# The gated delta rule stage of a two-block model: spread rows, masks and the order of the recurrence

## The chip, the core and the metric

The kernel runs on one core of a Trainium2 chip. The metric is the device time of one execution in microseconds (us), lowest is best. TensorE (PE) does the matrix products and writes to PSUM, whose eight banks hold 512 fp32 columns each. VectorE (DVE), ScalarE (ACT) and GpSimd (POOL) do elementwise work, SyncE (SP) issues most DMAs.

## The reference

One sequence of 512 tokens with 16 meta tokens goes through a two-layer block (attention, a short convolution, two MLPs), and then, without the meta tokens, through one hybrid mixer. That mixer normalizes its input, projects it, and runs two branches beside each other: a differential attention with 4 heads, and a gated delta rule with 4 heads of dimension 128 in 8 chunks of 64 tokens. Both outputs are gated and go through one output projection. The change concerns the delta rule:

```
g = cumsum(g within a chunk)
decay = exp(where(tril, g[:, None] - g[None, :], -inf))
lower = where(strict, (k * beta) @ k.T * decay, 0)
u, w = triangular_solve(lower + I, [v * beta, k * beta * exp(g)])
qk_intra = where(tril, q @ k.T * decay, 0)
for each chunk:                                  # state is 128x128 per head
    v_new = u - w @ state
    o = (q * exp(g)) @ state + qk_intra @ v_new
    state = state * exp(g_last) + (k * exp(g_last - g)).T @ v_new
```

## The kernel before

Everything is computed in transposed form, channels on partitions and the 512 tokens along a row. All loops are written out by hand for each engine, and engines wait for each other by counting semaphores (`gd.wait(engine, name, count)`). No scheduler moves anything. PE works in the order written.

The stages of the last 300 us, in the order of PE:

- The input projection of the mixer (L430 products). Its last tile gives `rows`, the 4-partition row quantities of the delta rule, one row for each head.
- The differential attention, four heads c = 0 to 3 (`dif_act`, `dif_dve`, `dif_pe`; products L1833, L1835, L1841, L1865). Between its steps ACT and DVE compute the rows in `rows_act` and `rows_dve`: beta, exp(g), -beta exp(g), exp(g_last - g) and the scan G. With k = 0 (in head 0) ACT has 7 operations, with k = 2 (end of head 1) 9. In head 3 `rows_pe` (L1676) turns four rows into columns with 16 products of 4 columns, and DVE copies them to `gcol`.
- `gdn_pe`, `gdn_act`, `gdn_dve`, `gdn_pool`, the delta rule. Keys and values are turned (L2068, L2076) and scaled by columns: `KDEC` and `X1` on ACT (L2175, L2181), `X2` on DVE (L2249), each in 4 operations a head (one for each block of 128 tokens, called j).
- The exponents of the decays: PE spreads row G of head h over 128 partitions with a selection matrix, `hsel` (L2083, 4 rows, fp32), and adds the mask by four products with the identity (L2085, fp32). ACT takes the exponential (L2186).
- The products q k and k k (L2091, L2097), multiplied on DVE with the decays (L2254, L2257). The spread rows beta (L2101) and exp(g) (L2104) multiply them and the queries (L2261, L2264).
- The inverse of the triangular matrix by levels of doubling blocks: POOL masks the first level for all heads (L2240), DVE forms `TT` (L2268), PE turns it (L2108), and then come five levels of three groups of products (L2125, L2132, L2135). POOL masks for heads 0 and 1, DVE for heads 2 and 3 (L2277).
- The solutions (L2140, L2143), evicted by ACT.
- The recurrence over 8 chunks. In each chunk PE does, for all four heads, the product w state (L2152, bank 4+h) and the query product (L2153, bank h). Then DVE adds u to make `vn` (L2306), and PE does for each head the update of the state (L2160, bank 4+h) and the output part (L2162, bank h). These two have only 64 rows, partitions 0 to 63 in an even chunk and 64 to 127 in an odd one. DVE forms the new state (L2315).
- The normalization of the outputs: ACT squares, PE sums over partitions (L2168), ACT takes the inverse root, DVE multiplies (L2326, L2328), ACT and DVE split the result in a high and a low part. The output projection (L430) starts with the blocks of the attention (k = 4 to 7), and its first tile waits until `o_scaled`, signalled by L2326, has released its bank.

A plain fp32 product is two instructions in the profile (two pairs of weight load and matmul). One whose operands are declared fp32r (a rounded form) is one, and the kernel gets precision back by splitting into high and low parts.

## Time and profile before

| | |
|---|---|
| median of 3 runs | 1817.6 us (1816.02 to 1818.84) |
| profiled execution, own time | 1817.29 us |
| its span | 1815.5 us |
| PE busy | 1743.3 us, 96% |
| DVE, ACT, POOL busy | 885.2, 633.8, 142.4 us |
| chain that ended last, by engine | PE 91%, DVE 4%, ACT 3% |
| TensorE clock granted, mean | 0.967 of full |

The profiled execution took 1.79 us more than its span, and lies 0.3 us under the median. A matmul's end is modelled, so starts are better to read than ends. "PEclk" is the granted clock, 1.00 for 2.4 GHz and 0.50 for 1.2 GHz. Times in rows are counted from the start of the span.

### The profile page before, as it was taken

The numbers are of one execution on the slowest core, as the hardware profiler recorded it, in microseconds if no ns is written. First come the engines' busy times: TensorE is split into PE (matmuls) and PEld (weight loads), VectorE is DVE, ScalarE is ACT, GpSimd is POOL, SyncE is SP. The second block draws the span as 40 slices with busy tenths as digits, with TensorE's granted clock in tenths as the row PEclk, the third lists the DMA queues.
The fourth block names the chain that finished last, engine by engine and source line by source line (L and its number), as shares of the span: only waits on it lengthen the run. The fifth ranks groups of instructions, "written<-read, shape, count | busy, mean of one in ns | idle before, by whom it ended". The sixth has DMA issues, their size and how long they took to land.

```text
span 1815.5 us, 27268 instructions
## 1 busy us (share of the span) xinstructions
PE 1743.3 (96%) x11417; PEld 1511.6 (83%) x11417; DVE 885.2 (49%) x1193; ACT 633.8 (35%) x980; POOL 142.4 (8%) x151
## 2 busy tenths in 40 slices
PE   7999898989999999999999999999999999889998
PEld 6997566789999999999887888888877886666987
DVE  5533346455343333565566333444566477534362
ACT  4523424423232222321233222323344465641222
POOL 1000000032000000220023000000231000003200
PEclk9999898999999999999999999999999999967999
DMA  5240001022232222222223232322364760001001
GB/s 177 71 96 5 7 1 47 2 71 93 93 93 93 93 83 89 87 89 93 93 93 93 94 99 97 103 94 92 95 88 70 94 94 18 1 11 47 1 24 70
DMA packets 137545, 129.57 MB, mean 71 GB/s; under 512 B 17633, under 2 KB 135512, under 8 KB 137452
## 3 DMA queue, kind: packets, MB, share of 16 engines
q1 hardware_dynamic: 137250, 128.18, 26.0%
q8 instruction: 69, 1.13, 0.3%
q14 instruction: 24, 0.20, 0.0%
q10 hardware_dynamic: 202, 0.06, 0.0%
HBM read 126.14 MB, written 2.10 MB: 71 GB/s over the span
## 4 chain that ended last, share of the span: by engine, by line
PE 91%; DVE 4%; ACT 3%; issue 1%; SPq 1%; DMA 0%; ACTq 0%; DVEq 0%
PE ps L430 71%; PE ps L859 3%; PE ps L756 1%; PE ps L739 1%; PE ps L1865 1%; PE ps L1090 1%; PE ps L2125 1%; PE ps L2135 1%; PE ps L2132 1%; PE ps L1152 1%; PE ps L2152 0%; PE ps L2160 0%; PE ps L764 0%; SPq L2376 0%; PE ps L2083 0%
## 5 line engine op out<-in xcount | busy, mean ns | idle before, releaser
L403 ACT ACTIVATE w_hi<-raw 128x1024 fp32r<-128x1024 f32 (+1 forms) x227 | 239.3, 1055 | 825.8 <-PE ps L430 819.6
L430 PE MATMUL ps<-x_hi,w_hi 128*128 128x258 f32 (+4 forms) x1640 | 450.5, 327 | 3.6 <-DVE x_lo L450 2.8
L430 PE MATMUL ps<-x_lo,w_hi 128*128 128x258 f32 (+4 forms) x1640 | 444.4, 323 | 0.0
L430 PE MATMUL ps<-x_hi,w_lo 128*128 128x258 f32 (+4 forms) x1640 | 443.4, 323 | 0.0
L411 DVE TENSOR_TENSOR w_lo<-raw,w_hi 128x1024 fp32r<-128x1024 f32 (+1 forms) x227 | 294.6, 1299 | 96.8 <-ACT w_hi L403 96.7
L430 PEld LDWEIGHTS ps<-x_hi,w_hi 128*128 128x128 f32 (+2 forms) x1640 | 273.4, 188 | 34.7 <-issue 3.8
L430 PEld LDWEIGHTS ps<-x_lo,w_hi 128*128 128x128 f32 (+2 forms) x1640 | 272.3, 187 | 28.0 <-issue 2.4
L430 PEld LDWEIGHTS ps<-x_hi,w_lo 128*128 128x128 f32 (+2 forms) x1640 | 272.2, 188 | 25.7
L430 PE MATMUL ps<-a_hi,w_hi 128*128 128x258 f32 (+1 forms) x1024 | 281.8, 326 | 10.3 <-issue 10.3
L430 PE MATMUL ps<-a_hi,w_lo 128*128 128x258 f32 (+1 forms) x1024 | 281.6, 326 | 0.0
L430 PE MATMUL ps<-a_lo,w_hi 128*128 128x258 f32 (+1 forms) x1024 | 281.4, 326 | 0.0
L430 PEld LDWEIGHTS ps<-a_hi,w_hi 128*128 128x128 f32 x1024 | 172.3, 190 | 28.5 <-issue 11.2
L430 PEld LDWEIGHTS ps<-a_hi,w_lo 128*128 128x128 f32 x1024 | 172.6, 190 | 17.1
L430 PEld LDWEIGHTS ps<-a_lo,w_hi 128*128 128x128 f32 x1024 | 172.5, 190 | 17.0
L1313 DVE TENSOR_TENSOR h<-h,ps 128x512 f32<-128x512 f32 (+1 forms) x88 | 60.7, 689 | 229.5 <-PE ps L430 229.5
L1380 DVE SCALAR_TENSOR_TENSOR tmp<-ps,scale_bc 128x516 f32<-128x516 f32 (+1 forms) x64 | 44.4, 693 | 172.1 <-PE ps L430 162.2
L460 POOL TENSOR_TENSOR acc<-h 128x516 f32<-128x516 f32 (+1 forms) x4 | 4.2, 1045 | 874.2 <-DVE h L1313 874.2
L463 POOL TENSOR_TENSOR acc<-acc,sq 128x516 f32<-128x516 f32 (+1 forms) x28 | 59.8, 2136 | 2.2
L450 DVE SCALAR_TENSOR_TENSOR x_lo<-h,vec,x_hi 128x516 fp32r<-128x516 f32 (+2 forms) x40 | 58.1, 1466 | 0.1
L859 PE MATMUL ps<-prob,v_one 128*128 128x512 f32 (+4 forms) x160 | 49.9, 455 | 4.4 <-ACT prob L872 4.4
L859 PEld LDWEIGHTS ps<-prob,v_one 128*128 128x128 f32 (+1 forms) x160 | 30.5, 207 | 23.7 <-issue 11.5
L2240 POOL TENSOR_TENSOR gdn_LB<-gdn_LT,gdn_masks 128x128 f32<-128x128 f32 x56 | 24.3, 473 | 291.8 <-DVE gdn_LT L2261 262.4
(397 smaller groups left out, 1868.7 us busy)
## 6 DMA issues: line engine op xcount, KB each, us to landing
raw<-in_w_mlp_up SPq DMA_DIRECT2D x32, 1024.0 KB, 5.4
raw<-in_w_mlp_down SPq DMA_DIRECT2D x32, 1024.0 KB, 4.9
raw<-in_w_in SPq DMA_DIRECT2D x16, 1024.0 KB, 9.1
raw<-in_w_in_conv SPq DMA_DIRECT2D x12, 1024.0 KB, 5.1
raw<-in_w_in_attn SPq DMA_DIRECT2D x8, 1024.0 KB, 5.2
raw<-in_w_out_attn SPq DMA_DIRECT2D x4, 1024.0 KB, 5.0
raw<-in_w_out_conv SPq DMA_DIRECT2D x4, 1024.0 KB, 5.0
raw<-in_w_out SPq DMA_DIRECT2D x4, 1024.0 KB, 5.2
```

Of the source, the lines that this page charges most:

```text
L403: act.activation(dst, panel_view(p)[:, :, o:o + w], ACT.Copy).then_inc(w_hi_ok, 1)
L411: dve.tensor_tensor(lo, panel_view(p)[:, :, o:o + w], hi.bitcast(F32), ALU.subtract).then_inc(w_lo_ok, 1)
L430: ins = pe.matmul(pair_of_banks[t % 2][0:m, b, 0:c], w[:, k, :], x[:, k, x0:x0 + c], start=(k == order[0] and n == 0), stop=(k == order[-1 ...
L450: dve.scalar_tensor_tensor(x_lo[:, c, f:], h[:, c, f:], col(*nm.gain(c)), x_hi[:, c, f:].bitcast(F32), ALU.mult, ALU.subtract).then_inc(x_ ...
L463: pool.tensor_tensor(acc[:, f:], acc[:, f:], sq[:, f:], ALU.add).then_inc(acc_ok, 1)
L739: ins = pe.matmul(slot[0:nq, x, c0:c0 + nk], q, k, start=(n == 0), stop=(n == last))
L756: ins = pe.matmul(slot[0:nk, x, c0:c0 + nq], k, q, start=(n == 0), stop=(n == last))
L859: ins = pe.matmul(ps[:, 6 + x, 512 - n:512], v_one[0:rows, j, c % 4, 64 * x:64 * x + P], prob[0:rows, x, p0:p0 + n], start=(j == 0), stop= ...
L1090: ins = pe.matmul(slot[:, bank, 0:wd], a, b[:, x0:x0 + wd], start=(k == 0 and n == 0), stop=(k == len(w) - 1 and n == 2))
L1313: dve.tensor_tensor(like(dst, width), like(dst, width), in_psum(pair_of_banks[t % 2], width), ALU.add).then_inc(evicted, 1)
L1380: dve.scalar_tensor_tensor(like(tmp[:, j % 2, 0:w], w), in_psum(pair_of_banks[(t0 + j) % 2], w), 0.0, like(scale_bc[:, f:], w), ALU.max, A ...
L2240: ins = pool.tensor_tensor(blk(LB, h, j), blk(LT, h, j), gmask[:, 1 + i, :], ALU.mult)
```

## The change

Eight things change:

1. `row_cols` is a cleared 128x512 tile with one row quantity of all heads at partitions 0, 32, 64 and 96. `rows_pe` turns it with four whole 128x128 transpositions instead of 16 small products.
2. The rows to be spread (G, beta, exp(g)) are kept as an fp32r high part at partitions 0 to 3 and a low part at 32 to 35 of cleared tiles. `hsel` now has 64 rows, loaded whole (256 KB, before 8 KB). A spreading product is one 64-row fp32r instruction. For this ACT does two more copies of 4x512 in k = 0 and two in k = 2, and DVE three more 4x512 operations in k = 3. POOL clears the four tiles and casts `hsel` (`rows_pool`, behind its last work of the attention).
3. The mask of the exponents is added by one bf16 product of 512 columns, with operands made at the start of the kernel.
4. The column scalings of `X2` and `X1` are one 128x512 operation a head, both on DVE. `X2` waits for ACT's `scaled`.
5. The masks of the levels and `TT` are one 128x512 operation a head (POOL and DVE), the table or the identity read four times.
6. The recurrence runs in nine turns. In turn t heads 0 and 2 are at chunk t, heads 1 and 3 at chunk t-1. The first turn has only heads 0 and 2, the last only heads 1 and 3. In a turn all updates of the state come before all output parts.
7. The outputs are normalized in the order 0, 2, 1, 3.
8. The first two tiles of the output projection wait for `o_scaled` of two heads (2h and 2h+1) instead of one.

```diff
+            pool.wait_ge(mm_done, T_OUT2)
+            for n, t in enumerate((G_R[:, :].bitcast(F32), BETA_R[:, :].bitcast(F32), EG_R[:, :].bitcast(F32), row_cols[:, :])):
+                pool.memset(t, 0.0).then_inc(gr["cleared"], 1)
+                pool.wait_ge(gr["cleared"], n + 1)
+            pool.wait_ge(s_tab2, 160)
+            pool.tensor_copy(hsel[:, :, :], hsel_in[:, :, :]).then_inc(gr["cleared"], 1)
...
-                act.activation(BETA, BETA, ACT.Exp, scale=-1.0)
+                link(act, "act", act.activation(BETA, BETA, ACT.Exp, scale=-1.0))
...
+                act.wait_ge(gr["cleared"], 4)
+                act.activation(BETA_R[0:4, :], BETA, ACT.Copy)
+                act.activation(row_cols[32:36, :], BETA, ACT.Copy)
...
-                act.activation(EG, G, ACT.Exp)
+                act.activation(G_R[0:4, :], G, ACT.Copy)
+                link(act, "act", act.activation(EG, G, ACT.Exp))
+                act.activation(EG_R[0:4, :], EG, ACT.Copy)
...
-                dve.scalar_tensor_tensor(NEG_BEG, EG, -1.0, BETA, ALU.mult, ALU.mult).then_inc(gr["last"], 1)
+                for x, t in ((G, G_R), (BETA, BETA_R), (EG, EG_R)):
+                    dve.tensor_tensor(t[32:36, :], x, t[0:4, :].bitcast(F32), ALU.subtract)
+                dve.scalar_tensor_tensor(row_cols[64:68, :], EG, -1.0, BETA, ALU.mult, ALU.mult).then_inc(gr["last"], 1)
...
-            for q, r in enumerate((NEG_G, BETA, NEG_BEG, KD)):
-                for j in range(4):
-                    ins = pe.matmul(misc[:, q * 16 + j * 4:q * 16 + j * 4 + 4], r[:, j * P:(j + 1) * P], tab["ident"][0:4, 0:4],
-                                    start=True, stop=True)
+            for j in range(4):
+                ins = pe.transpose(misc[:, j * P:(j + 1) * P], row_cols[:, j * P:(j + 1) * P], tab["ident"][:, :])
...
-                pe.matmul(A_bank(h), hsel[:, h * P:(h + 1) * P], G, start=True, stop=False)
-                for j in range(4):
-                    ins = pe.matmul(pblk(A_bank(h), j), tab["ident"][:, :], gmask[:, 0, :], start=False, stop=(j == 3))
-                ins.then_inc(gd.s["dt_pe"], 1)
+                pe.matmul(A_bank(h), hsel[0:64, h, :], G_R[0:64, :], start=True, stop=False)
+                pe.matmul(A_bank(h).rearrange("p (j q) -> p j q", j=4), id_r[:, :], neg_r[:, :].unsqueeze(1).broadcast_to([P, 4, P]),
+                          start=False, stop=True).then_inc(gd.s["dt_pe"], 1)
...
-                pe.matmul(B_bank(h), hsel[:, h * P:(h + 1) * P], BETA, start=True, stop=True).then_inc(gd.s["row_pe"], 1)
+                pe.matmul(B_bank(h), hsel[0:64, h, :], BETA_R[0:64, :], start=True, stop=True).then_inc(gd.s["row_pe"], 1)
...
-                for j in range(4):
-                    ins = pool.tensor_tensor(blk(LB, h, j), blk(LT, h, j), gmask[:, 1 + i, :], ALU.mult)
-                ins.then_inc(gd.s["lvl"], 1)
+                pool.tensor_tensor(blocks(LB[:, h, :]), blocks(LT[:, h, :]), every_block(gmask[:, 1 + i, :]), ALU.mult).then_inc(gd.s["lvl"], 1)
...
+        TURNS = [[(h, t - h % 2) for h in range(GH) if 0 <= t - h % 2 < NCH] for t in range(NCH + 1)]
+        OUT_ORDER = (0, 2, 1, 3)
...
-                    head = 2 * ((T_OUT2 + j) % 2)
-                    gd.wait(pe, "o_scaled", head + 1)
+                    for head in (2 * ((T_OUT2 + j) % 2), 2 * ((T_OUT2 + j) % 2) + 1):
+                        gd.wait(pe, "o_scaled", OUT_ORDER.index(head) + 1)
```

On PE, at the exponents of the decays, the order before is this (names are output, then operands; the last number is the output's shape and xN the count):

```order
L2083 MATMUL ps<-rows,hsel 128x512
L2085 MATMUL ps<-gdn_masks,t_ident 128x128 x4
L2083 MATMUL ps<-rows,hsel 128x512
L2085 MATMUL ps<-gdn_masks,t_ident 128x128 x4
L2083 MATMUL ps<-rows,hsel 128x512
```

and after the change, with the line numbers of the changed kernel:

```order
L2122 MATMUL ps<-rows_decay,hsel 128x512
L2123 MATMUL ps<-neg_r,id_r 128x512
L2122 MATMUL ps<-rows_decay,hsel 128x512
L2123 MATMUL ps<-neg_r,id_r 128x512
L2122 MATMUL ps<-rows_decay,hsel 128x512
```

The five products of a head have become two. The positions of the groups in the program are the same.

On PE, in the recurrence, a whole chunk of before (four heads, first the products with the state, then with `vn`):

```order
L2152 MATMUL ps<-gdn_state,gdn_T 128x128
L2153 MATMUL ps<-lat,gdn_state 128x64
L2152 MATMUL ps<-gdn_state,gdn_T 128x128
L2153 MATMUL ps<-lat,gdn_state 128x64
L2152 MATMUL ps<-gdn_state,gdn_T 128x128
L2153 MATMUL ps<-lat,gdn_state 128x64
L2152 MATMUL ps<-gdn_state,gdn_T 128x128
L2153 MATMUL ps<-lat,gdn_state 128x64
L2160 MATMUL ps<-gdn_LT,gdn_kdec 128x128
L2162 MATMUL ps<-gdn_AT,gdn_LT 128x64
L2160 MATMUL ps<-gdn_LT,gdn_kdec 128x128
L2162 MATMUL ps<-gdn_AT,gdn_LT 128x64
```

and the last two turns with the start of the normalization, after the change:

```order
L2197 MATMUL ps<-gdn_LT,gdn_kdec 128x128 x2
L2200 MATMUL ps<-gdn_AT,gdn_LT 128x64 x4
L2189 MATMUL ps<-gdn_state,gdn_T 128x128
L2190 MATMUL ps<-lat,gdn_state 128x64
L2189 MATMUL ps<-gdn_state,gdn_T 128x128
L2190 MATMUL ps<-lat,gdn_state 128x64
L2200 MATMUL ps<-gdn_AT,gdn_LT 128x64 x2
L2205 MATMUL ps<-gdn_LB,t_ones 128x512 x4
```

Updates (L2197) and output parts (L2200) now stand in two runs, and neighbours in such a run use different halves of the partitions.

## Rows read from the trace of the kernel before

**Rows 1.** Stretches: start and end, length, PE busy, granted clock, DMA share, GB/s.

```profile
1626.00:1632.00 6.00, 6.00 (x14) 0.50 0.00 0
...
1642.00:1646.00 4.00, 4.00 (x36) 0.94 0.02 4
...
1653.00:1657.00 4.00, 4.00 (x6) 0.50 0.00 0
```

**Rows 2.** The chain that ended last, in order: start us, us, what.

```profile
1543.77 0.52 ACT rows L1637
...
1549.85 4.14 PE ps L1865 x20
...
1599.21 7.00 PE ps L1676 x32
...
1625.57 2.04 PE ps L2083 x2
1627.61 2.00 PE ps L2085 x8
...
1641.63 4.02 PE ps L2091 x32
...
1652.89 6.84 PE ps L2104 x8
...
1660.44 5.32 DVE gdn_TT L2268 x16
...
1666.92 4.98 PE ps L2125 x32
```

**Rows 3.** PE in order of time: start us, us, what; fp32r products of 512 columns.

```profile
1761.24 0.39 PE L430 MATMUL ps<-a_hi,w_hi 128*128 128x512 f32 x1
1761.47 0.40 PE L430 MATMUL ps<-a_lo,w_hi 128*128 128x512 f32 x1
```

**Rows 4.** One chunk of the recurrence in order of time, PE and DVE.

```profile
1731.21 0.49 PE L2152 MATMUL ps<-gdn_state,gdn_T 128*128 128x128 f32 x2
...
1733.07 0.28 DVE L2306 TENSOR_TENSOR gdn_LT<-gdn_Y,ps 64x128 f32<-64x128 f32 x1 [0.17 <-PE ps L2152]
1733.14 0.29 PEld L2160 LDWEIGHTS ps<-gdn_LT,gdn_kdec 64*128 64x128 f32 x2
...
1733.66 1.69 DVE L2315 SCALAR_TENSOR_TENSOR gdn_state<-gdn_state,gdn_last,ps 128x128 f32<-128x128 f32 x4 [0.31 <-PE ps L2160]
...
1735.06 0.49 PE L2152 MATMUL ps<-gdn_state,gdn_T 128*128 128x128 f32 x2
```

**Rows 5.** ACT in order of time at the end of head 1.

```profile
1570.38 2.00 ACT L1650 ACTIVATE rows<-rows 4x64 f32<-4x64 f32 x8
...
1574.31 1.02 ACT L1880 ACTIVATE d_prob<-ps 128x1024 f32<-128x1024 f32 x1 [1.93 <-PE ps L1835]
```

**Rows 6.** DVE in order of time: a 128x512 operation with both operands repeated.

```profile
1554.14 0.69 DVE L1952 TENSOR_TENSOR d_shift<-ps,own_rows 128x512 fp32r<-128x512 f32 x1 [10.04 <-PE ps L1838]
```

**Rows 7.** POOL by line: count, busy us, mean ns of one, idle before.

```profile
L463 POOL TENSOR_TENSOR acc<-acc,sq 128x512 f32<-128x512 f32 x14 | 30.1, 2151 | 1.1
...
L2240 POOL TENSOR_TENSOR gdn_LB<-gdn_LT,gdn_masks 128x128 f32<-128x128 f32 x56 | 24.3, 473 | 291.8 <-DVE gdn_LT L2261 262.4 <-PE ps L2125 26.0 <-DVE gdn_TT L2268 3.4
...
L1804 POOL TENSOR_TENSOR dif_rot_b<-dif_g,dif_cos 128x512 f32<-128x512 f32 x8 | 10.4, 1300 | 37.0 <-ACT dif_g L1756 36.9
```

**Rows 8.** PE: 64-row fp32r products of two heads, alternating partition halves, 16 columns.

```profile
293.05 0.26 PE L739 MATMUL ps<-fox_hi,fox_lo 64*128 64x16 f32 x2
293.16 0.26 PE L739 MATMUL ps<-rope_k_one,rope_q_hi 64*128 64x16 f32 x2
```

**Rows 9.** The end of the normalization, DVE and PE in order of time.

```profile
1759.62 0.75 DVE L2326 SCALAR_TENSOR_TENSOR gdn_LB<-ps,vec,acc 128x512 f32<-128x512 f32 x1
...
1760.47 0.47 PE L430 MATMUL ps<-a_hi,w_hi 128*128 128x512 f32 x1 [3.24 <-issue]
...
1761.61 0.74 DVE L2326 SCALAR_TENSOR_TENSOR gdn_LB<-ps,vec,sq 128x512 f32<-128x512 f32 x1
```

More of the change, by code:

```diff
@@ L1622, in in2_dve @@
                     dif_largest_dve(dve, step[1], step[2])
-        gr = sems("rows", "sigmoid scan decays last turned saved")
+        gr = sems("rows", "cleared sigmoid scan decays last turned saved")
         CH, NCH, GH = 64, SEQ // 64, 4
@@ L1631, in program, with rows_pool @@
         gcol = at("gdn_cols", x_off + 32768, [P, 4, 4, GH])
+        row_hi_lo = [at(f"rows_{n}", off["w_hi"] + 2048 * i, [P, SEQ], F32R) for i, n in enumerate(("decay", "beta", "exp"))]
+        G_R, BETA_R, EG_R = row_hi_lo
+        row_cols = at("row_cols", off["w_lo"], [P, SEQ])
+        def rows_pool(pool):
+            pool.wait_ge(mm_done, T_OUT2)
[4 more added lines that the diff above has]
+            pool.tensor_copy(hsel[:, :, :], hsel_in[:, :, :]).then_inc(gr["cleared"], 1)
         def rows_act(act, k):
@@ L2144, in gdn_pe @@
                 ins.then_inc(gd.s["wu_pe"], 1)
-            for n in range(NCH):
-                j, r0 = n // 2, CH * (n % 2)
-                for h in range(GH):
+            for turn in TURNS:
+                for h, n in turn:
                     if n:
-                        gd.wait(pe, "state", GH * (n - 1) + h + 1)
-                        pe.matmul(B_bank(h)[:, 0:P], blk(TM, h, j), ST[:, h, :], start=True, stop=True).then_inc(gd.s["w_pe"], 1)
+                        gd.wait(pe, "state", nth(h, n - 1, hi=NCH - 1))
+                        pe.matmul(B_bank(h)[:, 0:P], blk(TM, h, n // 2), ST[:, h, :], start=True, stop=True).then_inc(gd.s["w_pe"], 1)
@@ L2153, in gdn_pe @@
                         pe.matmul(A_bank(h)[:, n * CH:(n + 1) * CH], ST[:, h, :], qk_a(h)[:, n * CH:(n + 1) * CH], start=True, stop=False)
-                for h in range(GH):
-                    gd.wait(pe, "vn", GH * n + h + 1)
+                for h, n in turn:
+                    r = slice(CH * (n % 2), CH * (n % 2) + CH)
+                    gd.wait(pe, "vn", nth(h, n))
                     if n == 0:
-                        gd.wait(pe, "wu", 2 * h + 1)
                         gd.wait(pe, "wu", 2 * h + 2)
@@ L2164, in gdn_pe @@
+                for h, n in turn:
+                    r = slice(CH * (n % 2), CH * (n % 2) + CH)
+                    ins = pe.matmul(A_bank(h)[:, n * CH:(n + 1) * CH], blk(LT, h, n // 2)[r, :], AT[r, h, n * CH:(n + 1) * CH], start=(n == 0), stop=True)
                     if n == NCH - 1:
                         ins.then_inc(gd.s["o_pe"], 1)
-            for h in range(GH):
-                gd.wait(pe, "o_sq", h + 1)
+            for n, h in enumerate(OUT_ORDER):
+                gd.wait(pe, "o_sq", n + 1)
@@ L2294, in gdn_dve @@
                         mask(i + 1, h)
-            for n in range(NCH):
-                j, r0 = n // 2, CH * (n % 2)
-                for h in range(GH):
-                    vn, u = LT[r0:r0 + CH, h, j * P:(j + 1) * P], YY[r0:r0 + CH, h, j * P:(j + 1) * P]
+            for turn in TURNS:
+                for h, n in turn:
+                    r = slice(CH * (n % 2), CH * (n % 2) + CH)
+                    vn, u = blk(LT, h, n // 2)[r, :], blk(YY, h, n // 2)[r, :]
                     if n == 0:
```

127 lines of the change are left out of this document (66 added, 61 removed).

## The prediction

> **What bounds the kernel now.** I read the page's slices first. PE is busy 9 tenths nearly everywhere, and only the slices from 1590 us on show a lower granted clock, so I went there with the stretches [rows 1]. They show a busy PE at 0.50, 1.2 GHz, while it spreads rows and adds masks (1626 to 1632), and again while it spreads exp(g) (1653 to 1657), and 0.94 in between, when the products q k begin. So part of the 96% is slow work. Then I read the chain that ended last [rows 2] from 1540 us to the end, to see which engine is late at each step of the change. It runs through ACT's rows in head 0 of the attention, through PE in the turning of rows (7.00 us), the exponents, and the spreading of exp(g) (6.84 us), through DVE in the identity step (5.32 us), and then through PE without a break. What is removed from these links is removed from the end, until the next engine is late. The order of time [rows 3 to 6, 8 and 9] gives pace and gaps.
>
> **The change, part by part.** Times are on the clock of the profiled execution.
>
> *Rows on ACT, head 0.* Two more copies of 4x512 and one more link. ACT is on the chain there, from 1543.77 [rows 2], and the next product of PE follows at 1549.85. The row L1637 of this size takes 0.52 us on the chain. Two copies and 0.2 for the link: +1.2 us. Bounds 0.8 and 2. PE then restarts at half clock for 20 instructions in 4.14 us, as now.
>
> *Rows on ACT and DVE, end of head 1.* ACT's last rows end at 1570.38 + 2.00 = 1572.38 and its next work starts at 1574.31, waiting for PE [rows 5]. Two copies and a link (1.2 us) fit in these 1.9 us. DVE, behind ACT, gets three more operations of up to 0.69 us [rows 6] and so ends its rows about 3.2 us later than now. What is queued behind them is the maximum for the next head, for which PE waits with the next scores. By my walk it still comes before ACT has need of the scores. I take 0, bounds 0 and 1.
>
> *Turning the rows.* 32 instructions in 7.00 us [rows 2] are 0.219 each, the half-clock pace. Four whole transpositions are one instruction each, 0.9 us, with 0.2 to land. PE goes on 5.9 us earlier. The value products behind it are unchanged. Bounds -5 and -6.1.
>
> *The exponents, q k, k k, spreading, masks.* This is one piece, from PE's start at 1625.57 to the first level at 1666.92 - 0.21 = 1666.7 [rows 2]. I walk through it.
> - DVE's first X2 starts at 1624.3 as now. One 128x512 operation from PSUM, with both operands repeated, takes 0.69 us [rows 6], where 4 smaller took 1.14. PE starts at 1625.05. X2 and X1 are 8 x 0.69 = 5.5 us on DVE, done at 1629.8. X1 leaves ACT, whose exponentials therefore begin with the first head.
> - A head's exponents take 4.04 us now (2.04 + 2.00) [rows 2]. Then they are two single instructions of 512 columns. These follow each other at 0.23 us at full clock [rows 3], so 0.43 at half, plus two changes of row mode. A change of mode shows as about 0.1 us: the 64-row products start at 1733.14, 0.27 us behind the last 128-row start, where the pace of such a pair is 0.17, and again at 1735.06 [rows 4]. So 1.06 a head, and 1629.3 at the end instead of 1641.6.
> - q k and k k are 64 instructions, 0.111 each at full clock (16 in 1733.14 to 1735.06, less the change of mode), 0.22 at half. Restarts in this trace stay at half for 3 to 4 us (4.14 for the 20 above). I take 4 us: 18 instructions by 1633.3, 46 more by 1638.4. DVE's last product with the decays ends 0.9 us later, 1639.3. PE's spreading products (8 x 0.23) hide under DVE.
> - DVE then has 4 + 4 operations (beta, exp(g)), 5.5 us: 1644.8. Here DVE becomes the bound, where now PE is with 6.84 us. Then the identity step, 4 operations. Now the 16 take 5.32, 1.33 a head, with POOL working on the same memory. Between 0.69 and 1.33 I take 1.0: 1648.8. The last transposition at half clock (4 x 0.22) gives 1649.8 for the first level instead of 1666.7: -16.9 us.
> - POOL: a head's mask as one operation. The nearest row is a two-input product of the same size, 1.30 us, the far one an in-place sum, 2.15, and now it is four of 473 ns [rows 7]. I take 1.3 to 1.6, since 128 columns in four parts give about that. POOL has its first mask from 1640.0 and is done with four by 1646, not late.
>
> Bounds of the piece: -14 (POOL slow and the clock late) and -20 (the clock up with the first exponents).
>
> On the mode changes, the Trainium skill ("TensorEngine Tiling (Array Packing)", Key Properties) says that changing the tiling mode drains TensorE, which speaks against mixing 64-row and 128-row products. The trace agrees, with 0.1 us for each change [rows 4]. On the identity step, the skill ("GPSIMD Engine Reference", Specifications) says that POOL's way to SBUF is shared with VectorE, with contention when VectorE has two SBUF inputs. The 1.33 us a head is the only row here that may show it.
>
> *The level loop and the solutions* have the same PE instructions, and PE is their bound throughout. 0.
>
> *The recurrence.* A chunk is 3.85 us, 1731.21 to 1735.06 [rows 4]: 32 instructions of 0.111, and two changes of mode. DVE's `vn` of the last head starts at 1733.07 and its state updates at 1733.66, four in 1.69. In the new order neighbours among the 64-row products use different halves. Two such products in different halves, each with a weight load of 128 columns, start every 0.11 us together [rows 8]: one takes 0.055, so both loads and products overlap. Here each product is two instructions on the same half, so the low part of one head goes beside the high part of the next: 16 instructions in 9 steps of 0.111, 1.0 us instead of 1.8. A full turn is then 1.93 + 1.0 + 0.1 = 3.0 us. The state of head 0 is ready 2.45 + 0.35 into the turn, just before PE needs it, and DVE has 4 x 0.29 + 1.69 = 2.85 us of work, so it doesn't bind either. First turn 1.0, second 2.1, six of 3.0, last 1.6: 22.8 us. Now it is 27.8: the first chunk without products with the state 1.9, six of 3.85, and the last without updates 2.8. -5.0, with +0.8 at the other end, where nothing overlaps and only the extra turn counts.
>
> *The end.* Now the first tile of the projection starts at 1760.47, just after the third `o_scaled` (1759.62 + 0.75 = 1760.37). The fourth is at 1761.61 + 0.74 = 1762.35 [rows 9]. This tile is on the bank of head 2, so in the new order it waits for heads 2 and 3, and head 3 is the fourth. That costs 2.0 us. Two squarings earlier give 0.2 back: +1.8, bounds +0.5 and +2.5.
>
> Behind PE's waits here stands nothing but the projection itself. POOL's clearing starts when the last projection tile is done, some 10 us before ACT asks for it in head 0. If it were late, ACT would stand still with the attention's exponentials behind it. The larger table (256 KB) and two casts at the start are off the chain. I cost them at 0, at most 0.5.
>
> Sum: 1.2 - 5.9 - 16.9 - 5.0 + 1.8 = -24.8. On 1817.29 of the profiled execution, which is 0.3 below the median of the runs, this gives 1792.5 us.
>
> **The rivals.**
> - *A. The 64-row products don't overlap.* In [rows 8] the operands alternate with each instruction, here only with every second, and each has a wait of its own. For it speaks that PE takes its instructions in order. Against it, that nothing orders different banks and halves. Price 5.8: 1798.3.
> - *B. Clock or POOL late in the middle.* The clock stayed at 0.50 from 1626 to 1641, though PE was busy with 128-row masks half of that time [rows 1]. Now 64-row fp32r and bf16 products come in their place, and if q k and k k all ran at half, 64 x 0.22 = 14.1 stands for 9.1: +5.0. POOL at 2.15 would have its two second-level masks at 1652.9, +2. About 1797.
> - *C. More is gained.* The clock rises before q k, and the identity steps take 0.69: -2 and -1.2, and a little at the end. 1788.5.
> - *D. Slower than before.* The clock stays at half in the level loop and the solutions, 1671 to 1725, because PE is idle for 5 us before it, while DVE works. Each us of that loop at half instead of full costs one us. From 25 us of it on the change is a loss; all 54 would give 1845. For it speaks that PE has more idle time ahead of the loop. Against it, that each restart in the trace came back to 1.00 within some 4 us once the products were dense, as from 1666.92 on (4.98 us for the first 32, then full pace).
> - *E. The change doesn't do what it says*, for the 512-column forms. If DVE took these as slowly as four small ones, 16 operations of 1.14 to 1.33 instead of 0.69 to 1.0 would cost 6: 1798.5. [Rows 6] is such a form at 0.69, so this is nearly out.
>
> **How the numbers follow.** Forecast 0.57 (its own range 1789.5 to 1795.5), A 0.13, B 0.14, C 0.12, D 0.03, E 0.01. The range has to hold A, B and C: 1786.5 to 1800.5. It leaves out D and the meeting of A with B. A difference under 0.2% (3.6 us) can't be told from none here. All cases but D are far beyond it: faster 0.96, same 0.01, slower 0.03.
>
> **What would show it.** The turning of rows: 4 instructions, under 1.3 us. The exponents: PE from first to last in 4 to 5 us. DVE busy without a gap in the products with beta and exp(g). The level loop unchanged. The recurrence with a turn of 3.0 us, updates in pairs 0.11 apart. PE idle before the projection for about 5 us instead of 3.24. Wrong it would be above all by a turn of 3.8 us, by a clock of 0.50 throughout q k and k k, or by a first level that waits for POOL.

## The result and the profile after

The changed kernel takes 1790.9 us (median of 4 runs, 1788.92 to 1791.87) against 1817.6 us (1816.02 to 1818.84): a ratio of 0.985, with a 95% interval of 0.9835 to 0.9869. The forecast was 1792.5 us. The profiled execution took 1791.16 us, 26.1 less than that of before; the forecast's sum was 24.8 less.

I cut both traces at the same places, all of them starts of PE's products, and compare the pieces (us):

| piece, from ... to ... | before | after | change | forecast |
|---|---|---|---|---|
| start of the span to the first sums of squares of head 0 | 1540.17 | 1540.04 | -0.1 | 0 |
| to the first value product | 9.68 | 12.63 | +3.0 | +1.2 |
| to the turning of the rows | 49.36 | 49.78 | +0.4 | 0 |
| to the first product of the exponents | 26.36 | 19.62 | -6.7 | -6.4 |
| to the first product of the levels | 41.14 | 22.07 | -19.1 | -16.4 |
| to the first product with a state | 60.65 | 59.08 | -1.6 | -0.9 |
| to the sums of the normalization | 26.16 | 22.62 | -3.5 | -4.1 |
| to the projection | 6.95 | 8.91 | +2.0 | +1.8 |
| to the end of the span | 55.03 | 54.65 | -0.4 | 0 |

(The forecast's -16.9 began with PE's start at 1625.05 instead of 1625.57; this 0.5 is put one line up here. Its -5.0 for the recurrence is split: the first turn, 1.0 instead of 1.9, is in the piece to the first product with a state, and the rest, 21.8 instead of 25.9, in the next.)

The chain that ended last, of the changed kernel, corresponds to [rows 2] (start us, us, what):

```profile
1552.67 4.58 PE ps L1887 x20
...
1602.45 1.13 PE ps L1697 x4
...
1625.09 3.57 PE ps L2129 x32
...
1635.35 2.39 DVE lat L2295 x4
1637.73 5.46 DVE gdn_TT L2298 x4
...
1644.35 4.31 PE ps L2163 x32
...
1734.75 45.91 PE ps L432 x192
```

The turning took 7.00 us and takes 1.13 now. The links of 2.04 and 2.00 for the exponents and of 6.84 for exp(g) are gone. DVE is the bound in their place, from 1633 to 1643, and the identity step on it has not become shorter: 5.46 us now, 5.32 before. Stretches as in [rows 1] say where the middle gained more than forecast:

```profile
1622.00:1633.00 11.00, 10.93 (x76) 9.04 (x77) 9.59 (x16) 4.23 (x16) 0.00 (x0) 1.00 0.01 1
1636.00:1644.00 8.00, 3.85 (x16) 3.05 (x17) 8.00 (x9) 2.50 (x7) 6.00 (x5) 0.50 0.75 249
```

(Columns: stretch, length, busy time of PE, its weight loads, DVE, ACT, POOL, then the granted clock, DMA share, GB/s.) The exponents and q k ran at 1.00, 2.4 GHz, where I had put the exponents and the first 4 us of q k at half. DVE is busy for all of the second stretch.

One turn of the changed kernel's recurrence in order of time, to be held against [rows 4]:

```profile
1714.77 0.49 PE L2189 MATMUL ps<-gdn_state,gdn_T 128*128 128x128 f32 x2
...
1716.70 0.76 PE L2197 MATMUL ps<-gdn_LT,gdn_kdec 64*128 64x128 f32 x8
...
1717.23 0.86 DVE L2342 SCALAR_TENSOR_TENSOR gdn_state<-gdn_state,gdn_last,ps 128x128 f32<-128x128 f32 x3 [0.31 <-PE ps L2197]
1717.25 0.60 PE L2200 MATMUL ps<-gdn_AT,gdn_LT 64*128 64x64 f32 x8
1717.78 0.38 PE L2189 MATMUL ps<-gdn_state,gdn_T 128*128 128x128 f32 x1
```

A turn is 1717.78 - 1714.77 = 3.01. The sixteen 64-row instructions take 1.08 of it, 1716.70 to 1717.78.

The end of the normalization, to be held against [rows 9]:

```profile
1729.78 0.74 DVE L2354 SCALAR_TENSOR_TENSOR gdn_LB<-ps,vec,sq 128x512 f32<-128x512 f32 x1
...
1733.79 0.74 DVE L2354 SCALAR_TENSOR_TENSOR gdn_LB<-ps,vec,sq 128x512 f32<-128x512 f32 x1
...
1734.75 0.76 PE L432 MATMUL ps<-a_hi,w_hi 128*128 128x512 f32 x1 [5.21 <-DVE gdn_LB L2354]
```

The first row is the second `o_scaled`, the second is the fourth. PE waits 5.21 us, until the fourth has ended.

### The profile page after: what moved, and what is told of

Its sections match the earlier page's. It is cut to its first block, busy times and chain, and to the rows that moved or that the text cites. A ratio compares the mean times of both kernels' runs of the same rounds, so it can differ in the third digit from the quotient of the medians.

```text
span 1789.4 us, 27043 instructions
## 1 busy us (share of the span) xinstructions
PE 1714.1 (96%) x11349; PEld 1493.2 (83%) x11349; DVE 884.9 (49%) x1146; ACT 632.1 (35%) x968; POOL 139.3 (8%) x116
## 4 chain that ended last, share of the span: by engine, by line
PE 90%; DVE 4%; ACT 4%; issue 1%; SPq 1%; DMA 0%; ACTq 0%; DVEq 0%
PE ps L432 72%; PE ps L861 3%; PE ps L741 2%; PE ps L758 2%; PE ps L1887 1%; PE ps L1092 1%; PE ps L2163 1%; PE ps L2173 1%; PE ps L2170 1%; PE ps L1154 1%; PE ps L2189 0%; PE ps L766 0%; PE ps L774 0%; PE ps L1098 0%; PE ps L1783 0%
## 5 line engine op out<-in xcount | busy, mean ns | idle before, releaser
L432 PEld LDWEIGHTS ps<-a_hi,w_lo 128*128 128x128 f32 x1024 | 172.6, 190 | 16.9
L432 PEld LDWEIGHTS ps<-a_lo,w_hi 128*128 128x128 f32 x1024 | 172.6, 190 | 16.9
L1387 DVE TENSOR_TENSOR a_lo<-tmp,a_hi 128x516 fp32r<-128x516 f32 (+1 forms) x64 | 44.5, 695 | 1.3 <-ACT a_hi L1364 0.9
```

What stands on the lines that cost most here:

```text
L432: ins = pe.matmul(pair_of_banks[t % 2][0:m, b, 0:c], w[:, k, :], x[:, k, x0:x0 + c], start=(k == order[0] and n == 0), stop=(k == order[-1 ...
L1387: dve.tensor_tensor(a_lo[:, j, 0:w], tmp[:, j % 2, 0:w], a_hi[:, j, 0:w].bitcast(F32), ALU.subtract).then_inc(a_lo_ok, 1)
```

## The experiments

Each starts from the changed kernel and was compared with the kernel before on the same chip. Runs of one kernel lie from 0.9 us (e9) to 8.7 us (e7) apart. Two things in the profiles move the whole without any edit. The stretch up to the first sums of squares, which lies ahead of what was edited in all but the last experiment, lasts 1537.6 to 1540.9 us. And in the middle the clock comes back early, ahead of the first product of the exponents, or late, behind the last; "early" and "late" mean this below, and the difference is 3.1 us. So what an edit is worth is read from the pieces of one profiled execution of each kernel, cut as above (the pieces at the two ends are left out; the last is 54.4 to 55.7 us in all of them):

| kernel | median us | ratio, 95% | to values | to turning | to exponents | to levels | to state | to sums | to projection |
|---|---|---|---|---|---|---|---|---|---|
| changed | 1790.9 | 0.9835 to 0.9869 | 12.63 | 49.78 | 19.62 | 22.07 | 59.08 | 22.62 | 8.91 |
| e1_one_head_wait | 1790.3 | 0.9844 to 0.9876 | 11.07 | 50.49 | 19.99 | 25.14 | 59.44 | 22.61 | 4.78 |
| e2_in_step | 1798.5 | 0.9884 to 0.9917 | 11.10 | 50.50 | 19.99 | 25.12 | 60.67 | 26.51 | 9.05 |
| e3_alternate | 1793.8 | 0.9859 to 0.9892 | 11.09 | 50.51 | 19.99 | 25.12 | 59.43 | 22.00 | 8.91 |
| e4_row_fp32 | 1800.5 | 0.9883 to 0.9919 | 11.08 | 50.49 | 19.98 | 31.06 | 59.87 | 22.62 | 8.91 |
| e5_mask_fp32 | 1795.3 | 0.9847 to 0.9892 | 11.08 | 50.51 | 19.98 | 29.80 | 58.82 | 22.62 | 8.90 |
| e6_turn_small | 1797.9 | 0.9874 to 0.9911 | 10.33 | 49.22 | 25.66 | 25.01 | 59.38 | 22.61 | 8.91 |
| e7_level_one_dve | 1792.1 | 0.9855 to 0.9888 | 12.64 | 49.80 | 19.60 | 20.49 | 58.30 | 22.62 | 8.91 |
| e8_beta_pool | 1787.1 | 0.9815 to 0.9844 | 9.66 | 49.33 | 19.57 | 22.08 | 59.05 | 22.62 | 8.91 |
| e9_small_forms | 1796.0 | 0.9870 to 0.9901 | 11.09 | 50.49 | 20.43 | 26.45 | 60.21 | 22.62 | 8.94 |
| e10_combined | 1785.4 | 0.9804 to 0.9838 | 9.67 | 49.37 | 19.56 | 20.45 | 58.30 | 22.00 | 4.78 |
| e11_filled | 1788.0 | 0.9829 to 0.9856 | 11.10 | 50.50 | 17.10 | 21.71 | 58.30 | 22.62 | 8.94 |
| e12_combined_filled | 1778.0 | 0.9768 to 0.9796 | 9.66 | 47.72 | 17.11 | 20.19 | 59.10 | 21.99 | 4.79 |

**The wait of the projection.**

```diff
-                    for head in (2 * ((T_OUT2 + j) % 2), 2 * ((T_OUT2 + j) % 2) + 1):
-                        gd.wait(pe, "o_scaled", OUT_ORDER.index(head) + 1)
+                    head = 2 * ((T_OUT2 + j) % 2)
+                    gd.wait(pe, "o_scaled", OUT_ORDER.index(head) + 1)
```

> The changed kernel, but the first two tiles of the output projection wait for o_scaled of one head (the one whose bank they write) instead of two. Theory: the wait for head 3 guards nothing, and PE is idle for it; in the trace of the changed kernel the second o_scaled ends at 1730.52 and the fourth at 1734.53, so the projection starts 4.0 us earlier, at about 1730.7. Its first 12 products belong to the attention and end about 1735.0, the 9 after them at 1737.1, later than the last a_lo (1736.65), so nothing else waits: 1790.9 - 4.0 = 1786.9 us. Rival 1: the last block's a_lo takes over part of it: 1788.5. Rival 2: something else holds the tile (low parts of the weights): 1790.9. Rival 3: the shorter idle time spares PE the half clock after it as well: 1785.

The projection began 4.1 us earlier (4.78 us behind the sums instead of 8.91). In the order of time:

```profile
1732.02 0.74 DVE L2354 SCALAR_TENSOR_TENSOR gdn_LB<-ps,vec,sq 128x512 f32<-128x512 f32 x1
...
1732.86 0.47 PE L432 MATMUL ps<-a_hi,w_hi 128*128 128x512 f32 x1 [1.08 <-issue]
1733.17 0.39 PE L432 MATMUL ps<-a_lo,w_hi 128*128 128x512 f32 x1
...
1738.17 0.50 PE L432 MATMUL ps<-a_hi,w_hi 128*128 128x512 f32 x1 [0.87 <-DVE a_lo L2349]
```

PE was idle for 1.08 us instead of 5.21, and its clock stayed up: products start 0.23 apart, where the first ones of the changed kernel started 0.43 apart. So the first 18 products were faster than I had reckoned, and the seventh of the eight blocks waited 0.87 for `a_lo`. From the sums to the end of the span it is 63.56 in the changed kernel and 59.82 with the edit: 3.7 us. The median shows only 0.6. In the profiled execution the middle was 3.1 longer than in the changed kernel's profile (25.14 for 22.07), which is a question for an experiment below.

**The order of the recurrence.** First all four heads are at the same chunk in a turn ("in step"); then the turns are skewed as in the change, but each output part stands behind its own update:

```diff
-        TURNS = [[(h, t - h % 2) for h in range(GH) if 0 <= t - h % 2 < NCH] for t in range(NCH + 1)]
-        OUT_ORDER = (0, 2, 1, 3)
+        TURNS = [[(h, t) for h in range(GH)] for t in range(NCH)]
+        OUT_ORDER = (0, 1, 2, 3)
```

> The changed kernel, but all four heads are at the same chunk in a turn (8 turns, normalization in the order 0, 1, 2, 3), as before the change. All updates of a turn still come before all output parts. Theory: the 64-row products of all heads then use the same partitions, none runs beside another, 16 of them take 1.8 us and not 1.0, and a turn is 3.75 to 3.85 us again: the recurrence 27.8 us instead of 22.8, and the whole 1790.9 + 5.0 + 0.2 = 1796.1 us. Rival 1: the gain came from the grouping of the updates and the faster state updates on DVE: 1791. Rival 2: half of it did: 1793.5.

```diff
                         pe.matmul(B_bank(h)[:, P:2 * P], blk(KDEC, h, n // 2)[r, :], blk(LT, h, n // 2)[r, :], ...)
-                for h, n in turn:
-                    r = slice(CH * (n % 2), CH * (n % 2) + CH)
                     ins = pe.matmul(A_bank(h)[:, n * CH:(n + 1) * CH], blk(LT, h, n // 2)[r, :], AT[r, h, n * CH:(n + 1) * CH], ...)
```

> The changed kernel with its nine skewed turns, but in a turn each head's output part follows its own update, as before the change. Theory: a product overlaps only with a direct neighbour on the other half of the partitions. Of 16 instructions four stand in a row on one half, so there are only 3 places of overlap in a turn: 13 steps of 0.111 = 1.44 us instead of 1.0, a turn of about 3.45 us, 1790.9 + 7 x 0.45 = 1794.1 us. Rival 1: PE overlaps them whatever their order: 1790.9. Rival 2: the overlap is lost wholly: 1796.5.

In step, a turn was 3.85 us again, and the pieces to the state and to the sums together are 5.1 us longer than in e1_one_head_wait, which also had the late clock (60.67 + 26.51 against 59.44 + 22.61), where 5.0 was expected. The same 64-row products, in step:

```profile
1714.70 1.16 PE L2197 MATMUL ps<-gdn_LT,gdn_kdec 64*128 64x128 f32 x8
...
1715.70 1.00 PE L2200 MATMUL ps<-gdn_AT,gdn_LT 64*128 64x64 f32 x8
1716.63 0.49 PE L2189 MATMUL ps<-gdn_state,gdn_T 128*128 128x128 f32 x2
```

They take 1.93 us instead of the 1.08 above. So the gain is the overlap, not the grouping, which this kernel kept. In the alternating order my theory fell: a turn of 3.45 was expected and 3.01 measured.

```profile
1717.10 0.50 PE L2197 MATMUL ps<-gdn_LT,gdn_kdec 64*128 64x128 f32 x4
...
1717.43 0.34 PE L2198 MATMUL ps<-gdn_AT,gdn_LT 64*128 64x64 f32 x4
...
1717.60 0.49 PE L2197 MATMUL ps<-gdn_LT,gdn_kdec 64*128 64x128 f32 x4
...
1718.19 0.38 PE L2189 MATMUL ps<-gdn_state,gdn_T 128*128 128x128 f32 x1
```

Heads 0 and 1 are done in the first 0.5, though four instructions in a row stand on one half of the partitions. Overlap does not need direct neighbours. The piece to the sums was even 0.6 shorter, mostly in the turns at the two ends (2.28 for 2.50 in the first of them, 1.68 for 1.96 in the last). My reading is that an output part no longer waits there for the other head's update; no row singles that out.

**What kept the clock low in the exponents.** The two parts of the exponents' change undone one at a time:

```diff
-                pe.matmul(A_bank(h), hsel[0:64, h, :], G_R[0:64, :], start=True, stop=False)
+                pe.matmul(A_bank(h), hsel[0:4, h, :].bitcast(F32), G, start=True, stop=False)
```

> The changed kernel, but row G is spread for the exponents by the 4-row fp32 product of before (two instructions); the mask stays one bf16 product. Theory: it is the 4-row products that kept the granted clock at 0.50 before (1625.57 to 1641), since they use 4 of the 128 rows. So the exponents run at half throughout: 2.04 for the row product as before and 0.6 for the mask, 2.65 a head, 10.6 us for four instead of 3.0 in the changed kernel, and the products q k begin at half, 1 us more: 1790.9 + 8.6 = 1799.5 us. Rival 1: the clock rises as in the changed kernel, the row product takes 1.0, a head 1.3: 1793.2. Rival 2: the mask products had kept the clock low, so this one rises after some us: 1796.

```diff
-                pe.matmul(A_bank(h).rearrange("p (j q) -> p j q", j=4), id_r[:, :], neg_r[:, :].unsqueeze(1).broadcast_to([P, 4, P]),
-                          start=False, stop=True).then_inc(gd.s["dt_pe"], 1)
+                for j in range(4):
+                    ins = pe.matmul(pblk(A_bank(h), j), tab["ident"][:, :], gmask[:, 0, :], start=False, stop=(j == 3))
+                ins.then_inc(gd.s["dt_pe"], 1)
```

This kernel also loads the fp32 mask table again, which PE waits for.

> The changed kernel, but the mask of the exponents is added by four fp32 products of 128 columns a head as before (8 instructions); the row stays one 64-row fp32r product. Theory (128-row products let the clock rise): at full clock 8 x 0.111 = 0.89 and 0.42 for the row, 1.3 a head instead of 0.74: 1790.9 + 2.3 = 1793.2 us. Rival 1: the clock stays at 0.50 in the exponents as it did before: 2.0 + 0.7 = 2.7 a head, and q k starts at half: 1799.7. Rival 2: the clock rises one step later than in the profiled execution of the changed kernel, as in three of the experiments: the first two or three heads at 2.7: 1796.

Both profiled executions ran the exponents at half clock throughout. The chain of e4_row_fp32, then that of e5_mask_fp32:

```profile
1621.35 2.04 PE ps L2122 x2
1623.39 0.54 PE ps L2123
```

```profile
1619.91 0.76 PE ps L2124
1620.67 2.00 PE ps L2126 x8
```

A head takes 2.54 us with the 4-row product and 2.72 with the four masks. e4 came out as expected (1800.5 for 1799.5), but the profile of e5 speaks against its theory: with no 4-row product in the stage, 128-row masks for three quarters of the time left the clock at 0.50 too, until q k began. (The lowest of its four runs, 1791.5, is where an early clock would put it, and has no profile.) The late clock is no property of the 4-row products. It came in e1, e2, e3, e6 and e9 as well, with the exponents of the changed kernel:

```profile
1614.00:1621.00 7.00, 4.61 (x21) 4.27 (x21) 3.08 (x5) 5.23 (x20) 0.00 (x0) 0.52 0.00 0
1621.00:1627.00 6.00, 6.00 (x14) 2.86 (x15) 3.93 (x7) 4.40 (x16) 0.00 (x0) 0.50 0.01 3
1627.00:1634.00 7.00, 7.00 (x60) 6.92 (x58) 4.84 (x7) 0.16 (x1) 0.00 (x0) 0.93 0.00 0
```

These stretches are of e1_one_head_wait. A head's exponents took 1.26 there instead of 0.74 at full clock, and the piece to the levels 25.1 instead of 22.1. In the changed kernel's own profile, in e7, e8 and e10 the clock was back before the exponents. What decides between the two was not settled: up to the projection the changed kernel and e1 are the same code, and they show both. What the new forms bring is that a late clock costs 3.1 us (25.1 for 22.1). With the old row product the same piece took 31.1, 9.0 more than the changed kernel with its early clock, and with the old masks 29.8, 7.7 more. In these two the clock was also late for longer, so 5.9 and 4.7 more than e1 is not the price of the forms alone.

**The turning of the rows.**

```diff
-            for j in range(4):
-                ins = pe.transpose(misc[:, j * P:(j + 1) * P], row_cols[:, j * P:(j + 1) * P], tab["ident"][:, :])
+            for q, r in enumerate((NEG_G, BETA, NEG_BEG, KD)):
+                for j in range(4):
+                    ins = pe.matmul(misc[:, q * 16 + j * 4:q * 16 + j * 4 + 4], r[:, j * P:(j + 1) * P], tab["ident"][0:4, 0:4],
+                                    start=True, stop=True)
```

> The changed kernel, but the rows are turned into columns by the 16 products of 4 rows (32 instructions) of before, from the rows at partitions 0 to 3, and ACT's copy of beta for the transposition is left out. Theory: 32 x 0.219 at half clock instead of 1.4 for four transpositions is 5.6 more, and 0.4 more in the value products behind, for which the clock comes later (6.51 against 6.09); 0.6 less in ACT's rows of head 0: 1790.9 + 5.4 = 1796.3 us. Rival 1: the transpositions hid something else that is late (the row for kd, the last value): under 3 us, 1793.5. Rival 2: the clock is late in the exponents too because of these products: 1799.5.

The turning took 7.00 us again (the piece to the exponents is 25.66 instead of 19.99, +5.7). In head 0, with one copy less on ACT, the first value product came 0.75 sooner, and PE then had less half clock: 4.01 and 2.23 for the two groups of 20 products, instead of 4.67 and 2.75. So this copy costs 2.0 us in all (11.08 + 50.50 against 10.33 + 49.22), of which ACT's own time, 0.75, is the smaller part.

**POOL and DVE on the same memory.** The second-level masks of heads 0 and 1 moved from POOL to DVE (POOL's loop leaves out i = 1, `mask(1, h)` runs over all four heads):

```diff
-            for i in range(6):
+            for i in (0, 2, 3, 4, 5):
...
-            for h in range(GH // 2, GH):
+            for h in range(GH):
                 mask(1, h)
```

> The changed kernel, but DVE computes the masks of the second level for all four heads, behind its identity steps, and POOL has none of that level. Theory: the identity step takes 1.38 us a head in place of 0.64 because POOL works on the same memory at the same time. Without POOL's two masks, the second to fourth step take 0.64 to 0.7 each, DVE is done with steps and masks by 1643.0, PE's transpositions (at half clock) end about 1642.0 instead of 1644.14: 1790.9 - 2.1 = 1788.8 us. Rival 1: the step is slow by itself (0.64 was a row of another kind): no gain, and one more mask of DVE ahead of the first level, 1791 to 1792. Rival 2: DVE is faster but the first level waits for the masks: 1790.

DVE in order of time, first the changed kernel, then this one:

```profile
1637.66 5.53 DVE L2298 TENSOR_TENSOR gdn_TT<-t_ident,gdn_LB 128x512 f32<-128x512 f32 x4
1643.10 1.28 DVE L2305 TENSOR_TENSOR gdn_LB<-gdn_LT,gdn_masks 128x512 f32<-128x512 f32 x2
```

```profile
1635.47 3.37 DVE L2298 TENSOR_TENSOR gdn_TT<-t_ident,gdn_LB 128x512 f32<-128x512 f32 x4
1638.75 2.49 DVE L2305 TENSOR_TENSOR gdn_LB<-gdn_LT,gdn_masks 128x512 f32<-128x512 f32 x4
```

In the second kernel only the first of the four steps, beside POOL's last first-level mask, takes 1.5 (from start to start); the three others take 0.60 each. In the changed kernel POOL works beside three of the four, and its groups of masks are these:

```profile
1633.73 4.94 POOL L2271 TENSOR_TENSOR gdn_LB<-gdn_LT,gdn_masks 128x512 f32<-128x512 f32 x4 [99.07 <-DVE gdn_LT L2292]
1639.30 3.33 POOL L2271 TENSOR_TENSOR gdn_LB<-gdn_LT,gdn_masks 128x512 f32<-128x512 f32 x2 [0.63 <-DVE gdn_TT L2298]
```

One by one, the three slow steps (DVE) and the masks beside them (POOL) of the changed kernel are:

```profile
1637.66 1.56 DVE L2298 TENSOR_TENSOR gdn_TT<-t_ident,gdn_LB 128x512 f32<-128x512 f32 x1
1637.41 1.25 POOL L2271 TENSOR_TENSOR gdn_LB<-gdn_LT,gdn_masks 128x512 f32<-128x512 f32 x1
...
1639.74 1.76 DVE L2298 TENSOR_TENSOR gdn_TT<-t_ident,gdn_LB 128x512 f32<-128x512 f32 x1
1639.30 1.65 POOL L2271 TENSOR_TENSOR gdn_LB<-gdn_LT,gdn_masks 128x512 f32<-128x512 f32 x1 [0.63 <-DVE gdn_TT L2298]
...
1641.42 1.76 DVE L2298 TENSOR_TENSOR gdn_TT<-t_ident,gdn_LB 128x512 f32<-128x512 f32 x1
1640.92 1.71 POOL L2271 TENSOR_TENSOR gdn_LB<-gdn_LT,gdn_masks 128x512 f32<-128x512 f32 x1
```

Each of the three steps ends 0.55 us after the mask beside it (1639.22 behind 1638.66, 1641.50 behind 1640.95, 1643.18 behind 1642.63). That is what two engines look like that take turns by whole operations, and not what two look like that slow each other in proportion.

The theory holds: the piece to the levels is 1.6 us shorter, and the next one 0.8, since PE found full clock in the first level. The median (1792.1) hides it, with runs from 1787.9 to 1796.6.

**The copies of beta.** They go to POOL, behind its cast of `hsel`, and DVE waits for them in k = 3:

```diff
-                act.wait_ge(gr["cleared"], 4)
-                act.activation(BETA_R[0:4, :], BETA, ACT.Copy)
-                act.activation(row_cols[32:36, :], BETA, ACT.Copy)
...
+            pool.wait_ge(gr["beta"], 1)
+            pool.tensor_copy(BETA_R[0:4, :], BETA).then_inc(gr["moved"], 1)
+            pool.wait_ge(gr["moved"], 1)
+            pool.tensor_copy(row_cols[32:36, :], BETA).then_inc(gr["moved"], 1)
```

> The changed kernel, but the two copies of beta (to the fp32r row and to row_cols) in head 0 are made by POOL instead of ACT. Theory: ACT is on the chain there; without 0.52 + 0.63 and the link (0.1 to 0.2) its rows end 1.3 us earlier and so does all behind: 1790.9 - 1.3 = 1789.6 us. Rival 1: PE restarts in another phase of its clock and this outweighs it either way (up to 1.5): 1788 or 1791. Rival 2: DVE, which now waits for POOL too, is late at the end of head 1: 1791.

The two pieces of head 0 are 9.66 and 49.33, as before the change (9.68 and 49.36): 2.6 us less than in e1 to e5 with the copies on ACT (11.08 and 50.50), of which 1.4 is ACT's time and 1.2 the clock of the products behind: the first 20 value products take 4.14 us instead of 4.67, the next 20 2.40 instead of 2.96. The five runs lie within 2.4 us, all of them below the changed kernel's lowest.

**The forms of 512 columns.** X2, X1, TT and the masks are done in four pieces a head again; this is the edit for X2:

```diff
-                dve.tensor_tensor(blocks(X2[:, h, :]), blocks(A_bank(h)), columns(nbeg_c, h), ALU.mult).then_inc(gd.s["x2"], 1)
+                for j in range(4):
+                    ins = dve.tensor_scalar(blk(X2, h, j), pblk(A_bank(h), j), gcolumn(nbeg_c, h, j), None, ALU.mult)
+                ins.then_inc(gd.s["x2"], 1)
```

> The changed kernel, but X2, X1, the identity step and the masks of the levels are again four operations of 128 columns a head (X1 stays on DVE). Theory: on DVE a head's X2 or X1 takes 1.14 instead of 0.60, so DVE comes to the products with the decays 4.3 us later than now (1626.0 in the changed kernel), PE's lead there absorbs some 2, and the first level starts about 2.4 us later; the identity step costs the same, since POOL and not the form sets it: 1790.9 + 2.4 = 1793.3 us. Rival 1: DVE has that slack, no difference: 1790.9. Rival 2: the forms carry a large part of the gain, 4 to 6 us: 1796.

Against e1, with the same late clock, it is 0.4 + 1.3 + 0.8 = 2.5 us longer up to the states, and 2.4 was expected. The way there was another in part: the identity step has 6.99 us on the chain instead of 5.46. POOL's 24 masks ran through beside it, 10.64 us without a break, which is the likely cause; it was not tested by itself.

**All together, and the clock itself.** First four edits at once: the projection waits for one head, the second-level masks are on DVE, the copies of beta on POOL, and each output part stands behind its own update.

> The changed kernel with four edits together: the projection waits for one head, the second-level masks are DVE's alone, POOL makes the copies of beta, and output parts follow their own update. If they add up: 3.7 (projection) + 1.8 (second-level masks) + 1.4 (copies) + 1.1 (less half clock behind the shorter wait in head 0) + 0.5 (order in the recurrence), by the profiles of the four alone: 1790.9 - 8.5 = 1782.4 us. Rival 1: the clock comes back late in the middle, 3.4 more: 1785.8. Rival 2: the edits get in each other's way (DVE bound at the first level): 1784.

The profiled execution took 1780.5 us, and the sum of the pieces from head 0 to the projection is 10.6 us less than in the changed kernel (184.1 for 194.7), where 8.5 was expected. Head 0 gave 3.4 (the changed kernel's profile had its clock at half there until 1543), the masks 2.4, the end 4.1 and the order 0.6. The median, 1785.4, missed the expected 1782.4. The five runs fall in two groups: 1779.5 and 1780.5, and 1785.4, 1785.9, 1786.6. Their middles are 6.0 apart. The mean granted clock of the runs on record goes with the groups, 0.978 and 0.979 in the first, 0.975 and 0.976 in the second. Over 1780 us that is 7 to 14 us more at half clock in the second group. Where these lie isn't shown, since only one of the five has a profile; a late clock in the middle alone would cost about 3 us of the 6.

Then products that nothing reads, placed where PE is idle:

```diff
+        def fill(pe, bank, n):
+            for _ in range(n):
+                pe.matmul(bank[:, 0:P], tab["ident"][:, :], tab["ident"][:, :], start=True, stop=True)
...
+            dz.wait(pe, "o_gated", 3)
+            fill(pe, misc, 16)
             dif_step_pe(pe, ("ot", 3))
```

> The changed kernel with products that nothing reads (identity by identity, fp32, 128 columns, 0.22 us each at full clock) in four idle stretches of PE: 12 ahead of the turning of rows, 16 ahead of the last values' turn, 8 ahead of the turn of the value block of head 1, 20 ahead of the turning of TT. Theory: the clock falls because PE is idle there; kept busy it stays at 1.00, the turning of rows takes 0.8 instead of 1.4, the value products 4.5 instead of 6.3, the first level 3.6 instead of 4.3, and the exponents always run at full clock: 3.9 us under the profiled execution of the changed kernel, and 3.4 more where it came back late. 1786 us. Rival 1: the clock falls anyway, and the added products only cost: 1791 to 1793. Rival 2: the work that gates PE (ACT, DVE) is unchanged, and what PE gains it waits for: under 1 us, 1790.

The granted clock stayed at 1.00 from 1594 to 1652 us; three of these stretches are:

```profile
1602.00:1608.00 6.00, 5.42 (x48) 5.00 (x47) 2.27 (x4) 1.34 (x3) 0.00 (x0) 1.00 0.01 3
1612.00:1618.00 6.00, 5.69 (x53) 5.53 (x52) 1.44 (x2) 5.93 (x25) 0.00 (x0) 1.00 0.04 11
1622.00:1633.00 11.00, 11.00 (x85) 9.97 (x85) 9.59 (x16) 2.66 (x11) 1.73 (x2) 1.00 0.01 2
```

The pieces to the exponents, to the levels and to the state are 2.5, 0.4 and 0.8 us shorter than in the changed kernel with its early clock, 3.7 in sum (3.9 expected), and 2.9, 3.4 and 1.1 shorter than in e1 with its late one. The median, 1788.0, is 2.9 below the changed kernel's and not at the expected 1786; the intervals of the two ratios overlap, so by the runs alone this gain is not clear of noise.

> The kernel e10_combined with the added products that nothing reads, as in e11_filled (12, 16, 8, and 12 ahead of the turning of TT), and two more stretches of them in head 0 of the attention: 7 ahead of the transposition of the maxima (nt), 12 ahead of the first value product. Theory: the clock is a matter of PE's idle stretches alone. The first values take 2.3 instead of 4.1 (-1.8), the products behind nt run at full clock (-1.2), the rest gives 3 us as in e11_filled against the profile of the changed kernel; by the profile of e10_combined (own time about 1780) the sum is 1774 us, and since no run can have the late clock the runs lie close together. Rival 1: the added products in head 0 end later than ACT and delay PE: 1776. Rival 2: what the middle gains is waited for (DVE bound): 1777 to 1778. Rival 3: no gain beyond the best run of e10_combined: 1780.

This is the fastest kernel here: 1778.0 us, 0.978 of before (0.9768 to 0.9796), clear of e10 without the added products (0.9804 to 0.9838). The first values took 2.50 instead of 4.14. It misses the expected 1774. The products ahead of nt brought nothing that the pieces show (to the values 9.66, and 9.67 in e10). And the 12 ahead of TT end 2.1 us before PE's wait does; the clock fell to 0.50 from 1633 to 1636 and the first level cost 0.8 more. The runs still span 5 us, and their mean granted clock goes from 0.981 (1780.4) to 0.985 (1775.5), so even here the clock is not the same in each run; where it differs isn't shown.

## Why the prediction was right

Every large term was of the forecast's kind and place. That the sum came within 1.3 us of the profiled execution is in part luck: two errors of opposite sign, both about the clock, hid each other, 2.2 us too little cost in head 0 and 3.0 too little gain in the middle.

- *Rows on ACT, head 0* (+1.2): mis-sized. ACT's own part was 1.4, of which the copies are 0.52 and 0.63. What I left out was the clock: PE waits longer, and what it does then runs longer at half clock, 1.2 more in e1 to e5. "PE then restarts at half clock for 20 instructions in 4.14 us, as now" is the sentence that failed. In the profiled execution the clock had also not come back by 1540 (the two instructions of the sums of squares take 2.00 us there, before 1.06), and head 0 costs 3.4.
- *End of head 1* (0): right. From the values of head 1 to those of head 2 it is 16.64 us before and 16.62 after.
- *Turning* (-5.9): right, and shown by undoing it (5.7).
- *The middle* (-16.9): the walk describes the profiles with the late clock, where the two pieces from the turning on are 45.1 instead of 67.5, -22.4 for the forecast's -22.8 (-5.9 and -16.9). Even there the steps differ: a head's exponents took 1.26 us instead of 1.06, and the clock came back 2 us into q k (e1), where I had taken 4. In the changed kernel's own profile the first half of rival C came true: the clock was up before the exponents, and these pieces gained 3.4 us more. The exponents took about 3 us from first to last instead of the 4 to 5 forecast. The second half of C (identity steps of 0.69) did not come true. The steps took 1.38 on the average, more than the 1.0 that I chose between the bounds, and DVE's products with beta and exp(g) took 0.60 instead of 0.69, which made up for half of it. An identity step takes 0.60 alone and 1.5 to 1.7 beside POOL. The Trainium skill ("GPSIMD Engine Reference", Specifications) says that POOL shares its interfaces to SBUF with VectorE and that they contend when VectorE has two SBUF inputs. The trace agrees: 0.60 us against 1.5 to 1.7 with two SBUF inputs, and 0.60 beside a working POOL with one input in PSUM.
- *POOL's mask* (1.3 to 1.6): 1.24 alone and 1.67 beside DVE. It was not late.
- *Level loop and solutions* (0): 0.7 less, since the first level found more of its time at full clock (4.31 us instead of 4.98).
- *Recurrence* (-5.0): right in cause, a turn of 3.01 for 3.0, and 4.4 in size. The first turn is 1.03 instead of 1.92, as forecast; the two short turns at the ends are 2.50 and 1.96, where I had 2.1 and 1.6. The level loop's 0.7 hid that. Rival A is out. That the low part of one head goes beside the high part of the next was too narrow a picture (e3).
- *The end* (+1.8): +2.0. The wait for the head whose bank the tile does not write guards nothing: without it the projection starts 4.1 us earlier (e1).
- *The rest of the projection* is 0.4 shorter, which I had not counted; that piece varies by 1.3 us among these kernels.
- A slip in rival D: all 54 us of the loop at half clock would give 1846.5, not 1845. Nothing rests on it.

## What to carry to other kernels

An operation put on an engine that PE waits for costs its own time and the half clock that the longer wait leaves behind. Here the second was nearly as large as the first (1.2 and 1.4 us), and the same copies on the idle engine cost nothing. Compare such kernels by pieces of the profile between fixed instructions: the clock's coming back early or late moved the middle by 3.1 us, more than several of the edits did. Ask of each wait which bank or tile it guards: one superfluous count was worth 3.7 us. Where PE idles for a few us ahead of dense work, products that nothing reads can be worth their place (e12 against e10: 7 us between the medians, 3.3 between the profiled executions).

## What the runs showed of the hardware

- 64-row fp32 products on the two halves of the partitions ran beside each other, 16 instructions in 1.08 us instead of 1.93 with all on one half (e2), also with four in a row on one half (1.09, e3).
- A 128x512 operation of DVE with both inputs in SBUF took 0.60 us from start to start alone (e7) and 1.5 to 1.7 beside a working POOL, whose own operation went from 1.24 to 1.67. Each slowed step of DVE ended 0.55 after POOL's operation. With one input in PSUM the same form took 0.60 beside a working POOL (1635.35, four in 2.39).
- With PE in dense work from 1620 or 1621 us on, the granted clock stayed at 0.50 for 10 us more in e5 and 14 us more in e4; in other kernels with the same code in the stage before, it was back before the exponents. What decides it stays open. With the idle stretches filled it did not fall there at all (e11).
